# A two-branch diffusion layer: gated outputs alternate through all heads, their stores move to ScalarE's queue, turned keys are copied behind the square

## The reference, cut to what matters

```python
q_dec = qc * jnp.exp(bc);  k_inv = kc * jnp.exp(-bc)
scores = jnp.where(mask, jnp.einsum('bnihd,bnjhd->bnhij', q_dec, k_inv), 0.0)
o_intra = jnp.einsum('bnhij,bnjhe->bnihe', scores, vc)
d_state = jnp.einsum('bnjhd,bnjhe->bnhde', k_to_end, vc)
# s = dec[..., None] * s + ds, chunk after chunk; o_inter = q_dec times the state before the chunk
o = (o_f + o_b[:, ::-1]).astype(x.dtype)
o = _rmsnorm(o, gla_norm_g).reshape(B, T, GLA_VDIM) * jax.nn.silu(gate_a)
y_a = o @ w_proj_a
```

## Time and profile before

| what | value |
|---|---|
| median of 3 runs | 2041.45 us (2041.24 to 2043.97) |
| the profiled execution, its own time | 2043.08 us |
| span of its profile | 2041.3 us |
| TensorE busy | 1946.9 us, 95% |
| VectorE busy | 997.1 us, 49% |
| ScalarE busy | 889.3 us, 44% |
| GpSimd busy | 576.2 us, 28% |
| mean granted TensorE clock | 0.982 |

### The profile page before, as it was taken

One profiled execution on the slowest core, in us unless ns is written; L12 is line 12 of the kernel. 1 busy time (PEld: TensorE's weight loads), 2 busy tenths in 40 slices (PEclk: granted clock), 3 DMA queues, 4 the chain that ended last, 5 costly groups with the idle time before them and its releaser, 6 DMA issues.

```text
span 2041.3 us, 30175 instructions
## 1 busy us (share of the span) xinstructions
PE 1946.9 (95%) x10585; PEld 1779.2 (87%) x10585; DVE 997.1 (49%) x1854; ACT 889.3 (44%) x1905; POOL 576.2 (28%) x643
## 2 busy tenths in 40 slices
PE   7899999999999999999999988779899999999997
PEld 2899999999999999999999776667798888898886
DVE  4778887764444345444443244445566422333333
ACT  3565667744445574344553245556643100211222
POOL 0236652323433314333330000000931022331122
PEclk9899999999999999999999998889899999999999
DMA  6578888777878887778889583552356666654433
GB/s 272 199 261 300 282 283 320 285 253 226 283 262 274 292 292 237 243 259 267 280 273 350 187 332 141 204 217 86 123 217 226 216 213 210 228 194 169 143 123 124
DMA packets 165243, 476.90 MB, mean 234 GB/s; under 512 B 14512, under 2 KB 51818, under 8 KB 156396
## 3 DMA queue, kind: packets, MB, share of 16 engines
q1 hardware_dynamic: 151276, 424.70, 60.4%
q10 hardware_dynamic: 13824, 50.34, 6.2%
HBM read 310.34 MB, written 155.20 MB: 228 GB/s over the span
## 4 chain that ended last, share of the span: by engine, by line
PE 85%; DMA 6%; DVE 3%; ACT 2%; POOL 2%; issue 1%; SPq 1%; POOLq 0%; ACTq 0%; DVEq 0%
PE bank L2020 48%; PE bank L2319 10%; PE bank L2271 10%; PE bank L2284 5%; PE bank L2148 2%; DMA og_dram<-og 2%; PE bank L2213 1%; PE bank L2137 1%; DMA w_raw<-in_w_in 1%; PE bank L2115 1%; POOL h_lo L970 1%; DMA v_ld<-v_dram 1%; PE bank L2044 1%; DMA x_st<-in_x 1%; PE bank L2060 1%
## 5 line engine op out<-in xcount | busy, mean ns | idle before, releaser
L2020 PE MATMUL bank<-h_hi,w_op 128*128 128x384 f32 x4032 | 1054.7, 337 | 11.2 <-DVE h_lo L1517 6.0
L2020 PEld LDWEIGHTS bank<-h_hi,w_op 128*128 128x128 f32 x4032 | 732.2, 188 | 15.1 <-issue 15.1
L2020 PE MATMUL bank<-h_lo,w_op 128*128 128x384 f32 x2016 | 675.1, 335 | 0.0
L2020 PEld LDWEIGHTS bank<-h_lo,w_op 128*128 128x128 f32 x2016 | 379.8, 188 | 0.0
L1511 DVE TENSOR_TENSOR w_op<-w_raw,w_op 128x512 fp32r<-128x512 f32 x240 | 187.3, 781 | 126.2 <-ACT w_op L1143 122.4
L1143 ACT ACTIVATE w_op<-w_raw 128x512 fp32r<-128x512 f32 x240 | 150.2, 627 | 161.6 <-PE bank L2020 154.1
L995 POOL TENSOR_TENSOR decs<-decs,qk_s 128x192 f32<-128x192 f32 x192 | 122.1, 672 | 333.7 <-ACT decs L1217 333.5
L2319 PE MATMUL bank<-in_a,pwa 128*128 128x512 f32 (+1 forms) x960 | 197.3, 368 | 0.0
L2319 PEld LDWEIGHTS bank<-in_a,pwa 128*128 128x128 f32 x960 | 167.3, 189 | 30.0
L2271 PE MATMUL bank<-ow,me_hi 128*128 128x512 f32 x576 | 177.3, 389 | 0.0
L1566 DVE TENSOR_TENSOR outs<-bank,u 128x384 f32<-128x384 f32 x180 | 99.5, 553 | 118.8 <-PE bank L2020 117.9
(11 more groups left out here) (222 smaller groups left out, 2647.4 us busy)
## 6 DMA issues: line engine op xcount, KB each, us to landing
w_op<-wt_dram SPq DMA_DIRECT2D x192, 512.0 KB, 5.4
wt_dram<-w_op ACTq DMA_DIRECT2D x96, 512.0 KB, 4.4
w_raw<-in_w_in SPq DMA_DIRECT2D x48, 768.0 KB, 5.9
w_raw<-in_w_in SPq DMA_DIRECT2D x24, 1024.0 KB, 6.8
qk_dec<-decs SPq DMA_DIRECT2D x48, 384.0 KB, 6.6
mg_dram<-outs SPq DMA_DIRECT2D x24, 768.0 KB, 6.8
swap<-qk_s SPq DMA_DIRECT2D x48, 192.0 KB, 5.6
v_dram<-outs SPq DMA_DIRECT2D x24, 384.0 KB, 4.8
```

The source lines that it names most:

```text
L2020: ins = pe.matmul(bnk, w_op[slot][:, part, k, :], h[:, j, k, :], start=(first and k == 0 and part == 0 and h is h_hi), stop=(k == HK - 1 a ...
```

## The change

There are four edits. (1) Blocks are numbered through all heads (`nth = NB * head + b`) and go to buffer `nth % 2`; the first gate of a block waits for the store of block `nth - 2`. (2) The 15 stores of heads 0 to 2 are issued by ScalarE, at the end of step s, where the block's last chunk was step s-2; those of head 3 stay on SyncE. (3) In the loads, those of head+2 are issued together after the head's last output, with no store between; for head 1 the other keys, the queries and the gates are loaded only after the first block of head 0 is gated. (4) On ScalarE, the copy of the turned key that opened step s+1 stands in step s, behind the square (and the kept copies) and ahead of the logarithm.

```diff
                     load_values(head, 0, LT - V_FIRST)
                     load_values(head, LT, NT)
-                load_queries(head)
...
             load_keys(1)
             load_first_values(1)
-            load_gates(1)
...
-                    if b == 3 and head + 2 < HEADS:
-                        sp.wait_ge(s_o, NT * head + V_FIRST)
-                        load_first_values(head + 2)
                     if b == NB - 1 and head + 2 <= HEADS:
                         sp.wait_ge(s_o, NT * head + NT)
                         if head + 2 < HEADS:
                             load_keys(head + 2)
+                            load_queries(head + 2)
...
-                    sp.dma_start(og_dram[...], og[:, b % 2, :, 0:n]).then_inc(s_ogst[b % 2], 16)
+                    if head == HEADS - 1:
+                        sp.dma_start(og_dram[...], og[:, (NB * head + b) % 2, :, 0:n]).then_inc(...)
+                    if b == 0 and head == 0:
+                        load_queries(1)
+                        load_gates(1)
+                    if b == 2 and head + 2 < HEADS:
+                        sp.wait_ge(s_o, NT * head + V_FIRST)
+                        load_first_values(head + 2)
...
             scale_queries(0)
+            k_out(run_term(0) + 1)
             for s in range(len(STEPS)):
-                run, others = run_term(s), kept_terms(s)
-                if run is not None:
-                    k_out(run + 1)
+                others = kept_terms(s)
...
                 for g in others[1:]:
                     k_out(g + 1)
+                if s + 1 < len(STEPS) and run_term(s + 1) is not None:
+                    k_out(run_term(s + 1) + 1)
                 act.wait_ge(s_sq2, s + 1)
...
                 act.activation(on[:, s % 2, :], o, ACT.Copy, scale=rms[:, 1:2]).then_inc(s_on, 1)
+                if s > 1:
+                    head, x = STEPS[s - 2]
+                    for b, (t0, n) in enumerate(BLOCKS):
+                        if head < HEADS - 1 and x == (t0 + n) // P - 1:
+                            t0, n = head_tokens(head, b)
+                            act.wait_ge(s_gt, s - 1)
+                            act.dma_start(og_dram[...], og[:, (NB * head + b) % 2, :, 0:n]).then_inc(...)
...
-                if x == BLOCKS[b][0] // P:
-                    stored = (2 if b % 2 else 3) * head + b // 2
-                    if stored:
-                        dve.wait_ge(s_ogst[b % 2], 16 * stored)
+                if x == BLOCKS[b][0] // P and nth > 1:
+                    dve.wait_ge(s_ogst[nth % 2], 16 * (nth // 2))
```

More of the change, by code:

```diff
@@ L756, in load_queries, with load_mixed @@
                 sp.dma_start(qd[n][:, :, :], qk_dec[head]).then_inc(s_ql[n], 16)
+            def load_mixed(g):
+                sp.dma_start(uf[:, g, :], u_dram[g]).then_inc(s_big[g], 16)
             def load_gates(head):
@@ L788, in _ @@
                             load_keys(head + 2)
+                            load_queries(head + 2)
                         else:
                             for g in range(GROUPS):
-                                sp.dma_start(uf[:, g, :], u_dram[g]).then_inc(s_big[g], 16)
+                                load_mixed(g)
                     sp.wait_ge(s_gt, NT * head + BLOCKS[b][0] // P + n // P)
-                    sp.dma_start(og_dram[2 * head:2 * head + 2, :, t0:t0 + n].rearrange("e p n -> p e n"),
-                                 og[:, b % 2, :, 0:n]).then_inc(s_ogst[b % 2], 16)
+                    if head == HEADS - 1:
+                        sp.dma_start(og_dram[2 * head:2 * head + 2, :, t0:t0 + n].rearrange("e p n -> p e n"),
+                                     og[:, (NB * head + b) % 2, :, 0:n]).then_inc(s_ogst[(NB * head + b) % 2], 16)
+                    if b == 0 and head == 0:
[4 more added lines that the diff above has]
+                        load_first_values(head + 2)
                 if head + 2 < HEADS:
@@ L808, in _ @@
             sp.dma_start(tab_c[:, :], io["tab_c"]).then_inc(s_tab_o, 16)
-            sp.wait_ge(s_ogst[0], 16 * 3 * HEADS)
-            sp.wait_ge(s_ogst[1], 16 * 2 * HEADS)
+            for n in range(2):
+                sp.wait_ge(s_ogst[n], 16 * (NB * HEADS // 2))
             sp.wait_ge(s_fst, 16 * 2 * HEADS)
@@ L1367, in _ @@
                 act.activation(on[:, s % 2, :], o, ACT.Copy, scale=rms[:, 1:2]).then_inc(s_on, 1)
+                if s > 1:
[4 more added lines that the diff above has]
+                            act.wait_ge(s_gt, s - 1)
+                            act.dma_start(og_dram[2 * head:2 * head + 2, :, t0:t0 + n].rearrange("e p n -> p e n"),
+                                          og[:, (NB * head + b) % 2, :, 0:n]).then_inc(s_ogst[(NB * head + b) % 2], 16)
             act.wait_ge(s_tab_e, 16)
@@ L1769, in gate @@
                 n, b = head % 2, min(x // 4, NB - 1)
+                nth = NB * head + b
                 c = chunk_at(head, x)
                 at = c * P - head_tokens(head, b)[0]
-                if x == BLOCKS[b][0] // P:
-                    stored = (2 if b % 2 else 3) * head + b // 2
-                    if stored:
-                        dve.wait_ge(s_ogst[b % 2], 16 * stored)
+                if x == BLOCKS[b][0] // P and nth > 1:
+                    dve.wait_ge(s_ogst[nth % 2], 16 * (nth // 2))
                 dve.wait_ge(s_ot, s + 1)
                 for e in range(2):
-                    ins = dve.scalar_tensor_tensor(og[:, b % 2, e, at:at + P], bank[7][:, e * P:e * P + P],
+                    ins = dve.scalar_tensor_tensor(og[:, nth % 2, e, at:at + P], bank[7][:, e * P:e * P + P],
                                                    cols[:, C_GG + e:C_GG + e + 1], ga_ld[n][:, e, c * P:c * P + P],
```

## The result

The changed kernel takes 2005.88 us (median of 4 runs, 2005.09 to 2007.41), the kernel before beside it 2042.71: ratio 0.982, interval 0.9803 to 0.9837. It is 36.8 us faster, where 55 were forecast, and 2 us above the range of 1977 to 2004.

A forecast was written before the change was run, and what follows sets the result against it. TensorE, busy 95% of the span, was taken as the bound, with waits in attention to remove. 38.6 + 10.6 + 13.0 - 6.0 - 1.0 = 55.2 us off 2043.08 gave 1987.9, forecast as 1986 us against the runs' median; range 1977 to 2004.

The forecast's parts named there:

- Buffers alternate through all heads: Head borders: three gate waits of 31.6 us go, with 7.0 us of slow clock behind them, 38.6 us gross.
- Stores on ScalarE's queue: Head borders: block 3's store lands 6.5 us after issue, a 1.3 us wait each; 6 us booked as lost.
- A landing of 10 us or more: Sign of being wrong, for the stores that ScalarE issues at the head borders.
- the sum that fits, 6.9 us of turns: Border store, one 2 KB row alternating with one 9 KB load row: lands after 6.9 + 1.4 = 8.3 us.
- stores stay behind the loads: Rival at the head borders: the store lands about B + 15.5 (B: head's last output's end); 2008 us, chance 0.12.
- My sum without the 6 us: The whole kernel's forecast gains, 38.6 + 10.6 + 13.0 - 1.0 us, leaving out the 6.0 booked for late border stores.
- The issue itself: ScalarE issuing 15 stores, 0.33 us or a little more each: 1 us lost in all, bounds 0 to 5.
- Loads in one go: Head 0, step x = 4: head 1's values land 8.4 us sooner, the 7.5 us wait goes; 10.6 us gained.
- Turned keys: Steps with one kept term fall from 3.46 to 3.05 us by the copy's new place; 13 us gained.
- The rival with no gain: Copy's new place brings nothing because ScalarE's chain bounds the step: 1999 us, chance 0.12.
- the slower one: Rival: logarithm behind the waiting copy makes `on` late in each of 72 steps; 2051 us at 0.9 a step, chance 0.03.
- What is late next: Fourier branch after the last head: GpSimd's folds have 13.0 us of slack, 8.5 used, still hidden by 4.5.

The follow-up runs named there:

- alternate_alone: The kernel before with only the buffers alternating through all heads, everything else as it was: 2006.2 us, ratio 0.9818 to the kernel before.
- store_rows_4k: The changed kernel with og_dram laid out so that stores run in 128 rows of 4 KB, not 256 of 2 KB: 1999.5 us, ratio 0.9795 to before.
- first_loads_as_before: The changed kernel with head 1's other keys, queries and gates loaded in the order before the change: 2017.4 us, ratio 0.9872 to the kernel before.
- store_step_earlier: The changed kernel with ScalarE's stores issued one step earlier, still on ScalarE's queue: 1985.2 us, ratio 0.9719 to the kernel before.
- loads_wait_for_store: The changed kernel with SyncE starting the border loads only when block 3's store, still on ScalarE's queue, has landed: 1986.1 us, one run.

## Why the prediction was wrong, point by point

*Buffers alternate through all heads.* Right: 38.6 us gross were forecast, alternate_alone gives 36.6 and takes the borders from 38.7 to 0.

*Stores on ScalarE's queue.* This is the step that failed: "6.5: a wait of 1.3 us at each of the three borders, 4 us, and 2 us more for a clock that may fall. I book 6 us of 38.6 as lost again." The place, the waiter and the limit were right: 5.2 us from issue to need were reckoned, 5.6 were there (13.2 less a wait of 7.6). The landing was 13.2, 9.4 and 12.7 us, beside 6.5, and the loss 24.2 us beside 6, so 18.2 of the 18.4 us that are missing (55.2 forecast, 36.8 measured). A landing of 10 us or more was named ahead as a sign of being wrong. Two things were mis-sized.

The first is the share. I took the value near ScalarE's stores of the first stage, as if they had shown how such a store passes loads. But their rows are 4 KB, and over that stretch SyncE's queue took 43% of the DMA engines' time and ScalarE's own 34%, so they often had no full stream beside them; a border store has twice the rows, and each waits for a load row of 0.35 us. I had the sum that fits, 6.9 us of turns, in a side sentence, and did not let it set the value.

The rule of the Trainium skill ("DMA: Bandwidth & Descriptors", section "Queues, rings and completion order") that each engine takes turns between queues held in the main. The section has an engine drain a whole packet, typically some 9 to 17 descriptors, before it switches; here, counted over all 16 engines together, the unit between long rows was about one row (273 and 288 load rows to 256 of the store at borders 1 and 3), and the measurement decides.

The second is the begin: I counted 1.4 us for issue and receipt, and the store's first row moved 3.7 to 4.1 us after its issue behind loads, 0.9 without them. Nothing in my sum stood for what was already queued in front. Measured, the landings are 3.7 + 8.3 + 1.2, 4.0 + 4.6 + 0.8 and 4.1 + 7.7 + 0.9 us (begin, rows, receipt). An estimate by turns, if each of the 16 engines has 16 of the rows, is 4 + 16 x (0.09 + 0.35) + 1 = 12 us for borders 1 and 3; at border 2 many load rows are shorter.

The rival "stores stay behind the loads" had the size nearly right (2008 us) for another reason: it reckoned with 15.5 us from the border, and the store landed 14.7 us from the first load's issue. What tells them apart is store_rows_4k: more bytes to a row brought it forward, with the loads in front unchanged.

*The order was the point.* I saw that block 3's store moves from ahead of the loads to behind them, and treated that as a matter of queue speed. The two kernels that put it ahead again, on either queue, run at 1985 to 1986 us. My sum without the 6 us would have said 1980 for them: the other terms together were some 5 us too large (36.6 of 38.6 for the buffers, about 12 of 13 for the copy in kernels without ScalarE's stores, the rest not assigned).

*The issue itself.* 1 us booked, 0 measured, as long as the copy is not behind it.

*Loads in one go.* Right: 10.6 us forecast, 3.66 us instead of 14.23 in that step, 11.5 us by first_loads_as_before. The margin is nothing: in the two kernels at 1985 to 1986 us the wait for these values is back with 0.4 and 0.7 us.

*Turned keys.* Right: steps of 3.05 us forecast and 3.04 measured, 2.61 in x = 4. 13 us forecast; 13.8 by the squares (4.6 a head), 11.6 to 13.4 in the experiments without ScalarE's stores. The rival with no gain and the slower one did not come: `on` was never late by more than 0.2 us.

*What is late next.* Right: TensorE didn't wait for GpSimd's folds in the changed kernel, nor in the two at 1985 to 1986 us.

## What to carry to other kernels

Where a store must land soon, issue it ahead of the large loads; here that held on either queue. A store issued behind them paid twice: for what was already queued, and then one long row of the loads for each of its own rows. Count rows, not only bytes. When a move changes who issues a transfer, write down what it was ahead of before and what it is behind after.

Measure edits of a bundle apart. Here the first edit alone gave as much as the bundle, two more parts gave some 12 us each, and one took 20.

## What the runs showed of the hardware that was not expected

The first row of a store that has no loads in front moves 0.9 us after its issue (store_step_earlier, loads_wait_for_store). Behind loads that another queue began 1.5 us earlier it is 3.7 to 4.1 us in the changed kernel, and 142 to 162 load rows (1.3 to 1.5 MB) begin in between.

Rows of 2 KB of a store and of 9 and 18 KB of loads run nearly one to one, counted over all engines, so 0.52 MB took 8.3 us beside 2.9 MB at border 1. The same 0.52 MB in 4 KB rows took 5.6 us.

With a border wait of 7.6 us the granted clock is 0.73 over the 12.5 us that hold it, partly the 1.2 GHz level, and 0.55 in the 5.0 us of work right behind it. At the second border, with a wait of 3.7 us, the loss by squares (5.6) still exceeded the wait by 1.9.
